# A three-layer routed-expert chain on one core: gate batches in pairs behind two slabs, and seams with row sums from the residual add and centred squares on ScalarE

## The reference, cut to what matters

```python
q = (xt @ w_q).reshape(T, PEER_HEADS, 2, PEER_HALF)
s = jnp.einsum('thpd,hpkd->thpk', q, sub_keys)
s_top, i_top = lax.top_k(s, PEER_TOPK)
...
best, pos = lax.top_k(cand, PEER_TOPK)
eid = jnp.take_along_axis(cand_id, pos, axis=-1)
gate = jax.nn.softmax(best, axis=-1)
act = jax.nn.gelu(jnp.einsum('td,thkd->thk', xt, u_tab[eid]), approximate=False)
out = jnp.einsum('thk,thkd->td', gate * act, v_tab[eid])
```

```python
h = layer_norm(DN_ALPHA * h + mix, ln_g, ln_b)   # (x - mean) * rsqrt(var + 1e-5) * g + b
n = rmsnorm(h, g)                                # x * rsqrt(mean(x*x) + 1e-6) * g
```

## Time and profile before

| | |
|---|---|
| median of 3 runs | 3086.1 us (3082.06 to 3093.37) |
| profiled execution | 3086.6 us, its span 3084.8 us |
| mean granted TensorE clock | 0.985 of full speed |
| busy in the span | PE 2974.1 us (96%), DVE 2069.3 (67%), ACT 1598.8 (52%), POOL 927.5 (30%) |
| chain that ended last | PE 87%, DVE 6%, ACT 2%, POOL 2% |
| DMA | 508.56 MB, 165 GB/s in the mean |

### The profile page before, as it was taken

The page is one execution under the profiler, slowest core; times in us unless marked ns, Lnnn a source line. Parts: engine busy times, 40 slices in busy tenths (PEclk is TensorE's granted clock), DMA queues, the critical chain, the costliest instruction groups (busy, mean ns, idle before and its releaser), DMA issues.

```text
span 3084.8 us, 66506 instructions
## 1 busy us (share of the span) xinstructions
PE 2974.1 (96%) x22893; PEld 2685.8 (87%) x22893; DVE 2069.3 (67%) x4318; ACT 1598.8 (52%) x2606; POOL 927.5 (30%) x378
## 2 busy tenths in 40 slices
PE   7899999999999989999999999899899999999998
PEld 6799999877788879999997778688799999977887
DVE  4369377888555554937788865675429477788755
ACT  3355443577454435553447755464545544477644
POOL 5578600000004647880000000155768820000000
PEclk9899999999999999999999999899999999999999
DMA  5345544455654325554445565443445544455564
GB/s 193 123 171 184 176 159 163 160 167 164 214 191 161 132 83 177 179 184 162 157 160 166 163 207 192 143 130 123 150 151 179 184 168 157 163 162 165 180 195 157
DMA packets 141401, 508.56 MB, mean 165 GB/s; under 512 B 16992, under 2 KB 18016, under 8 KB 140912
## 3 DMA queue, kind: packets, MB, share of 16 engines
q1 hardware_dynamic: 141296, 507.16, 49.8%
HBM read 506.05 MB, written 1.05 MB: 164 GB/s over the span
## 4 chain that ended last, share of the span: by engine, by line
PE 87%; DVE 6%; ACT 2%; POOL 2%; issue 1%; DMA 1%; SPq 1%; DVEq 0%; ACTq 0%; POOLq 0%
PE col L496 15%; PE col L498 14%; PE col L497 14%; PE acc L496 12%; PE acc L497 11%; PE acc L498 11%; PE acc L612 2%; PE col L612 2%; POOL w_lo L453 2%; ACT w_hi L717 1%; PE acc L581 1%; DVE work L1714 0%; DVE acc L958 0%; DVE pairs_of_gate L1144 0%; PE acc L1578 0%
## 5 line engine op out<-in xcount | busy, mean ns | idle before, releaser
L453 POOL TENSOR_TENSOR w_lo<-ring,w_hi 128x1024 fp32r<-128x1024 f32 x374 | 927.3, 2492 | 1560.5 <-ACT w_hi L717 1558.2
L717 ACT ACTIVATE w_hi<-ring 128x1024 fp32r<-128x1024 f32 x941 | 993.4, 1056 | 585.0 <-PE acc L498 477.4
L496 PE MATMUL col<-x_hi,w_hi 128*128 128x256 f32 (+1 forms) x3976 | 1143.0, 287 | 15.0 <-DVE x_lo L941 6.1
L497 PE MATMUL col<-x_lo,w_hi 128*128 128x256 f32 (+1 forms) x3976 | 1124.9, 283 | 0.0
L498 PE MATMUL col<-x_hi,w_lo 128*128 128x256 f32 (+1 forms) x3976 | 1123.6, 283 | 0.0
L453 DVE TENSOR_TENSOR w_lo<-ring,w_hi 128x1024 fp32r<-128x1024 f32 x567 | 692.1, 1221 | 221.4 <-ACT w_hi L717 221.4
L496 PEld LDWEIGHTS col<-x_hi,w_hi 128*128 128x128 f32 x3976 | 757.0, 190 | 22.3 <-issue 14.4
L498 PEld LDWEIGHTS col<-x_hi,w_lo 128*128 128x128 f32 x3976 | 757.5, 191 | 0.0
L497 PEld LDWEIGHTS col<-x_lo,w_hi 128*128 128x128 f32 x3976 | 753.8, 190 | 0.7
L496 PE MATMUL acc<-w_hi,c_hi 128*128 128x512 f32 x1664 | 668.3, 402 | 19.0 <-DVE c_lo L1049 10.3
L497 PE MATMUL acc<-w_lo,c_hi 128*128 128x512 f32 x1664 | 650.5, 391 | 0.0
(11 more groups left out here) (281 smaller groups left out, 2183.7 us busy)
## 6 DMA issues: line engine op xcount, KB each, us to landing
ring<-in_u SPq DMA_DIRECT2D x384, 512.0 KB, 3.2
ring<-in_v SPq DMA_DIRECT2D x384, 512.0 KB, 3.5
ring<-in_wq SPq DMA_DIRECT2D x48, 512.0 KB, 3.2
ring<-in_s_in SPq DMA_DIRECT2D x21, 512.0 KB, 3.5
ring<-in_c_in SPq DMA_DIRECT2D x16, 512.0 KB, 3.2
ring<-in_s_out SPq DMA_DIRECT2D x16, 512.0 KB, 3.5
ring<-in_s_gate SPq DMA_DIRECT2D x12, 512.0 KB, 3.5
ring<-in_s_conv SPq DMA_DIRECT2D x12, 512.0 KB, 3.5
```

The source lines that it names most:

```text
L453: eng.tensor_tensor(k.w_lo[s.slot][:, :], k.ring[s.slot][:, :], k.w_hi[s.slot][:, :].bitcast(F32), ALU.subtract).then_inc(k.lo[s.slot], 1)
L496: pe.matmul(out, a[0], b[0], start=start, stop=False, **kw)
L497: pe.matmul(out, a[0], b[1], start=False, stop=False, **kw)
L717: act.activation(k.w_hi[s.slot][:, :], k.ring[s.slot][:, :], ACT.Copy).then_inc(k.hi[s.slot], 1)
```

## The change

1. **Pairs.** In both passes PE takes two slabs and then two batches of gates. DVE's step takes two batches: both weighs, the one-hots of n+2 and n+3, then the splits (late: and coefficient rests) of slabs n+4 and n+5; the split of slab 3 goes ahead of the first weigh. The first late one-hots stand behind weigh 63.
2. **`row_tail`.** The third last slab is done whole; then tile 0 of the last two, then half 0 and then half 1 of tile 1. `tile_full` rises a second time when tile 1's half 0 is complete. The residual adds wait for each of these (`add_residual` now takes one half).
3. **Layer norm.** The residual add also gives its row sum (`accum_out`), from which a column operation makes the negative mean. ACT squares the centred rows (`centred_squares`), and their sums give the variance; the epsilon is the square root's bias. The two tiles' operations are interleaved on DVE by hand. ACT does four squares, two roots, and then the leads of slabs end+1 and end+2 (the latter behind `lead_x`, unless s is next).
4. **RMS seams.** DVE does all four residual adds first, then both norms (`finish_rms`). ACT squares both tiles ahead of the leads of end+1 and end+2.

```diff
@@ -615,17 +617,25 @@
         def gate_pass(late, slab):
-            for n in range(HEAD):
+            for n in range(0, HEAD, 2):
                 slab(n)
-                gates(Slab(n), late, wait=n >= SLOTS)
+                slab(n + 1)
+                for b in (n, n + 1):
+                    gates(Slab(b), late, wait=b >= SLOTS)
             with pe.Fori(0, TURNS - 1) as i:
-                for n in range(HEAD, HEAD + UNROLL):
+                for n in range(HEAD, HEAD + UNROLL, 2):
                     slab(n, i * 2)
-                    gates(Slab(n, i * 2), late)
-            for n in range(BATCHES - UNROLL, BATCHES - 1):
+                    slab(n + 1, i * 2)
+                    for b in (n, n + 1):
+                        gates(Slab(b, i * 2), late)
+            for n in range(BATCHES - UNROLL, BATCHES - 2, 2):
                 slab(n)
-                gates(Slab(n), late)
-            gates(Slab(BATCHES - 1), late)
+                slab(n + 1)
+                for b in (n, n + 1):
+                    gates(Slab(b), late)
+            slab(BATCHES - 2)
+            for b in (BATCHES - 2, BATCHES - 1):
+                gates(Slab(b), late)
             slab(BATCHES - 1)
     def row_tail(self, end):
         k, pe = self.k, self.pe
-        for t in range(NT):
...
-                if t == NT - 1:
-                    ins.then_inc(k.used, 1)
-            if t == 0:
-                ins.then_inc(k.tile_full, 1)
+        last = end - 1
+        self.row_slab(Slab(end - SLOTS))
+
+        def part(n, t, half):
+            slot = n % SLOTS
+            cut, cols = slice(t * P, (t + 1) * P), slice(half * 512, (half + 1) * 512)
+            return self.split_matmuls(k.acc[t * 2 + half][:, :], (k.c_hi[slot][:, cut], k.c_lo[slot][:, cut]),
+                                      (k.w_hi[slot][:, cols], k.w_lo[slot][:, cols]), False, n == last,
+                                      skip_group_check=True)
+
+        for n in (last - 1, last):
+            pe.wait_ge(k.coef[n % SLOTS], k.rows_in_slot(Slab(n), 1))
+            self.slab_ready(Slab(n))
+            for half in range(2):
+                ins = part(n, 0, half)
+        ins.then_inc(k.tile_full, 1)
+        for half in range(2):
+            part(last - 1, 1, half).then_inc(*((k.used, 1) if half else (k.half_done, 1)))
+            part(last, 1, half).then_inc(*((k.used, 1) if half else (k.tile_full, 1)))
-    def std(self, src, dst):
+    def std(self, src, dst, bias=0.0):
         k, act = self.k, self.act
         self.w.next(k.var)
-        act.activation(dst, src, ACT.Sqrt).then_inc(k.std, 1)
...
+        act.activation(dst, src, ACT.Sqrt, bias=bias).then_inc(k.std, 1)
+
+    def centred_squares(self, t):
+
+        k = self.k
+        self.w.next(k.mean)
+        for half in range(2):
+            self.square(k.acc[t * 2 + half][:, :], 2 * t + half, bias=k.small[:, 20 + t:21 + t])
...
+        act.activation(view(k.big, JUNK, cols, p=rows), src, ACT.Square, bias=bias, accum_out=k.small[0:rows, 40 + n:41 + n])\
            .then_inc(k.sq, 1)
             self.tile_std(NT)
         self.split_lead(Slab(end))
         if name in RMS_AFTER:
-            self.tile_squares(0, bool(after))
-        else:
-            self.tile_std(0)
-        self.split_lead(Slab(end + 1))
-        self.split_lead(Slab(end + 2))
-        if name in RMS_AFTER:
-            self.tile_squares(1, bool(after))
+            for t in range(NT):
+                self.tile_squares(t, bool(after))
+            self.split_lead(Slab(end + 1))
+            self.split_lead(Slab(end + 2))
             if after:
                 self.lead_x(range(NT))
-        elif after != ("s",):
+            return
+        eps = k.small[:, 49:50]
+        for t in range(NT):
+            self.centred_squares(t)
+        for t in range(NT):
+            self.tile_std(t, eps)
+        if after != ("s",):
+            self.split_lead(Slab(end + 1))
             self.lead_x([0])
-            self.tile_std(1)
             self.lead_x([1])
+            self.split_lead(Slab(end + 2))
         else:
-            self.tile_std(1)
+            self.split_lead(Slab(end + 1))
+            self.split_lead(Slab(end + 2))
             for t in range(NT):
                 self.tile_squares(t, True)
             self.lead_x(range(NT), meta=True)
...
-    def add_residual(self, t, last, alpha, ready=None):
+    def add_residual(self, t, half, last, alpha, sums=False, ready=None):
         k, dve, own = self.k, self.dve, self.own
-        if t == 0:
+        if half == 0:
             self.w.next(k.tile_full)
-        else:
+        elif t:
             dve.wait_ge(k.used, last + 1)
-        for half in range(2):
-            acc = k.acc[t * 2 + half][:, :]
-            ins = dve.scalar_tensor_tensor(acc, k.h[:, t, half * 512:(half + 1) * 512], alpha, acc, ALU.mult, ALU.add)
-            if half == 0 or ready is None:
-                own.do(ins)
+        acc = k.acc[t * 2 + half][:, :]
+        ins = dve.scalar_tensor_tensor(acc, k.h[:, t, half * 512:(half + 1) * 512], alpha, acc, ALU.mult, ALU.add,
+                                       accum_out=k.small[:, 16 + 2 * t + half:17 + 2 * t + half] if sums else None)
         if ready is None:
-            own.join()
+            own.do(ins)
         else:
             ins.then_inc(ready, 1)
...
-        for t in range(NT):
-            self.add_residual(t, last, DN_ALPHA)
-            for half in range(2):
-                own.do(dve.bn_stats(stats[:, t, half, :], k.acc[t * 2 + half][:, :]))
+        means = self.w.count(k.mean)
+
+        def residual(t, half):
+            self.add_residual(t, half, last, DN_ALPHA, sums=True)
+
+        def minus_mean(t):
             own.join()
-            own.do(dve.bn_aggr(mean_var[:, t, :], stats[:, t, :, :].rearrange("p h s -> p (h s)")))
-            own.join()
...
-            if t == 0:
-                self.w.next(k.param[slot], 32)
-            for half in range(2):
-                acc = k.acc[t * 2 + half][:, :]
-                own.do(dve.scalar_tensor_tensor(acc, acc, mean_var[:, t, 0:1], gain[:, half * 512:(half + 1) * 512],
-                                                ALU.subtract, ALU.mult))
+            dve.tensor_scalar(k.small[:, 20 + t:21 + t], k.small[:, 16 + 2 * t:17 + 2 * t],
+                              k.small[:, 17 + 2 * t:18 + 2 * t], -1.0 / D, ALU.add, ALU.mult).then_inc(k.mean, 1)
+            self.w.skip(k.mean, 1)
+
+        def centre(t, half):
+            self.w.next(k.sq)
+            dve.wait_ge(k.mean, means + t + 1)
+            acc = k.acc[t * 2 + half][:, :]
+            own.do(dve.scalar_tensor_tensor(acc, acc, k.small[:, 20 + t:21 + t], gain[:, half * 512:(half + 1) * 512],
+                                            ALU.add, ALU.mult))
+
+        def variance(t):
+            dve.tensor_scalar(k.small[:, 4 + t:5 + t], k.small[:, 40 + 2 * t:41 + 2 * t],
+                              k.small[:, 41 + 2 * t:42 + 2 * t], 1.0 / D, ALU.add, ALU.mult).then_inc(k.var, 1)
+
+        residual(0, 0)
+        residual(0, 1)
+        minus_mean(0)
+        residual(1, 0)
+        self.w.next(k.param[slot], 32)
+        centre(0, 0)
+        residual(1, 1)
+        minus_mean(1)
+        centre(0, 1)
+        variance(0)
+        centre(1, 0)
+        centre(1, 1)
+        variance(1)
+        own.join()
+        scale(0)
+        scale(1)
...
+    def finish_rms(self, name, last):
+
+        k = self.k
+        slot = 0 if name == "s" else 1
+        for t in range(NT):
+            for half in range(2):
+                self.add_residual(t, half, last, 1.0, ready=k.rms_in if half else None)
+        for t in range(NT):
+            self.rms_norm(t, slot, name == "s")
...
         def early(n, i=None):
-            weigh(Slab(n, i), 0)
+            if n == 0:
+                split_rest(k, dve, Slab(late_u + SLOTS))
+            for b in (n, n + 1):
+                weigh(Slab(b, i), 0)
+            for b in (n + 2, n + 3):
+                if b < BATCHES:
+                    onehots(Slab(b, i), 0)
             if n + 2 < BATCHES:
-                onehots(Slab(n + 2, i), 0)
-            elif n + 2 == BATCHES:
+                for s in (n + 4, n + 5):
+                    split_rest(k, dve, Slab(late_u + s, i))
+            else:
                 onehots(Slab(0), 1)
-            if n < BATCHES - 1:
-                split_rest(k, dve, Slab(late_u + n + SLOTS, i))
...
+        def value(s):
+            split_rest(k, dve, s)
+            if s.turn is not None or s.base < first + BATCHES:
+                self.coef_rest(experts[:, s.index(first), :], s)
+
         def late(n, i=None):
-            weigh(Slab(n, i), 1)
+            if n == 0:
+                value(Slab(first + SLOTS))
+            for b in (n, n + 1):
+                weigh(Slab(b, i), 1)
+            for b in (n + 2, n + 3):
+                if b < BATCHES:
+                    onehots(Slab(b, i), 1)
             if n + 2 < BATCHES:
```

(28 more changed lines are left out.)

26 lines of the change are left out of this document (6 added, 20 removed).

## The result

The changed kernel took 3056.4 us (median of 4 runs, 3054.6 to 3062.3) beside 3085.0 for the kernel before (4 runs, 3082.1 to 3093.4): ratio 0.990, 95% interval 0.9886 to 0.9913. The forecast was 3055.5 in a range of 3043 to 3072. The profiled execution took 3062.3, the slowest of its four, with a span of 3060.5: 24.3 us less than the one of before.

What follows compares the result with a forecast made beforehand. The prediction took TensorE's stream, with the seams where it waits, as the bound; its terms summed to 31.1 us off the profiled 3086.6, giving 3055.5 us (chance 0.62), range 3043 to 3072.

Steps and rivals of the forecast that it cites:

- The switch: Gate passes: two gate blocks in a row save 0.09 us a pair, 16.7 us in all, bounds 0 and 22.
- Starts: Start of each early pass: slab 1 ahead of gates 0 covers TensorE's idle, 7.8 us gained, bounds 6 and 11.
- Hand-overs: Ends of the gate passes: VectorE's new order makes TensorE wait, 1.8 us lost early-to-late and 1.1 behind late passes.
- Rival d: Early-to-late hand-overs: the longer idle drops TensorE to 1.2 GHz in all three layers, 3060 us; chance 0.08.
- VectorE keeps up: Gate passes: VectorE needs 5.57 of 6.23 us per late pair, 5.13 of 6.42 early; spare 0.4, cost nil.
- Rival a: Late pass: VectorE becomes the bound if ScalarE's leads stand open, 3094 us with one, 3196 with both; chance 0.09.
- Rival b: Gate passes: pairs save nothing, as second-block waits or the slab-to-slab boundary cost what the switch did, 3072 us; chance 0.08.
- `row_tail`: Tails of row stages: the last slab's coefficients are needed 1.36 us later, which removes waits, 4.6 us gained together.
- Layer-norm seams: Seams behind ab, peer0 and c: fewer statistics and interleaved tiles gain 0.7 us each, 2.1 in all.
- Into s: Seam behind peer1: GpSimd's second split holds an SBUF addition for 1.96 us, 0.8 us lost; without the hold 1.5 gained.
- Behind s and the end: Seam behind s and kernel's end: adds first and squares ahead of leads gain 2.8 and 0.8 us.
- rival c: Seams and tails give nothing, as GpSimd holds small VectorE operations and accumulators cost 0.2: 9.5 us go, 3065 us; chance 0.13.

Runs made afterwards that it cites:

- e5: The changed kernel with TensorE's gate-pass loop cut behind a slab's 24 long matmuls instead of the gates' 24 short ones: 3049.7 us, ratio to before 0.9879.
- e2: The changed kernel with the pairs part undone (batches one by one), new row_tail and seams kept: 3075.8 us, ratio to before 0.9959.
- e3: The kernel before with row_tail's new order alone, norms and their order as before: 3091.2 us, ratio to before 1.0006.
- e6: The changed kernel with VectorE's order mended at both ends of a gate pass (weighs before split, coef_rest before late one-hots): 3049.1 us, ratio to before 0.9881.
- f3: The changed kernel with four more VectorE operations in each late pair, their results unread: 3148.2 us, ratio to before 1.0191.
- a0: The changed kernel unaltered, run again on a later occasion beside its parts: 3054.2 us, ratio to before 0.9887.

## Why the prediction was right, point by point

- **The switch.** The mechanism was right and the size was off. 0.09 x 186 = 16.7 was forecast and 11.3 measured, 12.8 with the odd early pass of before taken out. The 0.09 itself was about right: 0.08 late (6.36 - 6.28), 0.11 early (6.57 - 6.46). The step that failed is that the term had nothing for the turn of the loop, 0.09 in every third pair; with e5's 4.8 added the pairs give 17.6., from which the 0.79 came, lie outside the loop, so they could not show what its turn costs behind 24 short matmuls (e5). The estimate of 19.9 us by the Trainium skill ("TensorE: Matmul & The Clock Gate", LDWEIGHTS) is further off than the row's.
- **Starts.** 7.8 as forecast against the profile of before, 11.1 against e2's: that layers 1 and 2 kept full clock behind their idle was read from one execution, and the traces of e2 and e3 show half clock there. The upper bound of 11 was about right.
- **Hand-overs.** The order of VectorE's work was read rightly and the losses came out at 1.2 and 1.1 for 1.8 and 1.1. They were not the price of pairing: e6 takes them out. Rival d is out: the idle of 1.12 us left the clock at 1.00 in the five microseconds behind it in all three layers.
- **VectorE keeps up.** Right: 5.59 of 6.31 late (forecast 5.57 of 6.23), 146.91/182 x 6.49 = 5.24 early (forecast 5.13). f3 puts the room at 0.3 where 0.4 was given. Rival a is out, and f3 is what it would look like. Rival b is out as well: 6.28 for 6.36.
- **`row_tail`.** 4.4 for 4.6 in the profile after, but booked as if it stood alone; e3 shows that it is worth nothing without parts 3 and 4. And the step on c was wrong: it took the 1.38 us for VectorE in the earlier trace rows as lateness that six more matmuls would cover. It stood behind a `coef_rest` that took 2.52 us beside a GpSimd split, and in the new tail the last slab's is held so late that TensorE waits over 2 us for it in eight of twelve traces, where c loses 1.0 to 3.0 us in place of the 1.36 gained. That the profile after came near the sum was luck.
- **Layer-norm seams.** The term was twice too large, 2.1 for 1.0. The walk put tile 1's scale at E+5.35, +0.3 for accumulators; it came at E+5.87. The accumulator reads and the longer squares (0.69) are visible; how the 0.22 splits between them was not tried. The rest lies behind it: from the scale to the first matmul it is 3.62 us, where it was 3.43; TensorE now transposes both tiles in one go there, but whether that is the cause was not tried.
- **Into s.** This step failed. L1071 was to be held for two microseconds and wasn't: -0.8 forecast, +0.9 measured. The rule that a split holds such an addition stands (2.33 us in c); the walk had GpSimd start at E+5.0 and it started at E+5.9, while the addition came at E+8.1 and not E+7.5, so that it met the last 0.13 us of the first split. That it fell there was not foreseen, so the gain is luck; but the order of events is the same from one execution to the next: in the ten later traces of the new seams L1071 took 0.15 to 0.17 us. The question that the prediction left on the means is answered for this shape. In this seam, in all eleven traces with the new layer norms, the first mean (one column, one pointer scalar) starts inside a GpSimd split of 2.74 us and takes 0.21 us, as it does without one:

```profile
1963.37 2.74 POOL L455 TENSOR_TENSOR w_lo<-ring,w_hi 128x1024 fp32r<-128x1024 f32 x1 [581.61 <-ACT w_hi L730]
...
1965.19 0.21 DVE L1006 TENSOR_SCALAR small<-small 128x1 f32<-128x1 f32 x1
```

No split ran beside a variance.

- **Behind s and the end.** 3.1 and 0.9 for 2.8 and 0.8. With the tails and the layer norms this puts rival c out: seams and tails gave 10.3 us in the profile after.
- **Not in the prediction.** The held addition in c (-4.2 in this execution, nothing in seven others) and the half clock (+2.0). The total of 31.1 lies among the three measured differences, 28.6, 34.4 and 29.6, partly because errors of both signs met: the pairs and layer norms were booked 6.5 too high (5 with the odd early pass taken out), into s 1.7 too low, the starts up to 3.3 too low, and the half clock happened to help. The lower end of the range, 3043, is also 1.4 us below what its three named terms give (5.6, 3.2 and 2.3 from 3055.5: 3044.4).

## What to carry to other kernels

Price a pattern in the place where it will run: a pair outside a loop doesn't show what the loop's turn costs; here it cost 0.09 us behind 24 short matmuls, and nothing that shows behind 12 short ones or behind a slab. When work is reordered so that a producer finishes later, book it together with the consumer's order, since one without the other may be worth nothing. Before booking a wait as lateness, look at how long the awaited instruction took: 2.5 us for an operation that takes 0.43 elsewhere was a hold here, and the new order moved it rather than ended it. And at a hand-over, look at what stands ahead of the awaited instruction on its in-order engine before calling the idle a price of the change.

## What the runs showed of the hardware

- A VectorE operation of 128 x 8 numbers took 0.16 us when it started 0.04 us ahead of a GpSimd operation and 2.33 when it started 0.09 behind it; one of 128 x 256 numbers took 0.43 when it started 0.07 ahead and 2.61 when 0.01 behind. The Trainium skill ("SBUF — State Buffer", Who interferes with whom) says that an operation with two SBUF inputs contends with a GpSimd one that reads SBUF, and that "issue order, not op shape, decides who blocks"; the traces agree, and show that a seam's or a tail's time can hang on less than a tenth of a microsecond, in the same kernel.
- The clock behind a seam is not a property of the kernel. The same stretches of the same kernel, the start of c and the start of peer1, had granted clocks of 0.87 and 0.67 in the first execution:

```profile
952.00:965.00 13.00, 11.19 (x81) 0.87 0.26 83
...
1132.00:1145.00 13.00, 12.14 (x72) 0.67 0.26 82
```

and the other way round in a0:

```profile
952.00:965.00 13.00, 11.55 (x69) 0.67 0.25 83
1128.00:1141.00 13.00, 12.20 (x89) 0.87 0.29 91
```

In the balance of these two traces they are worth 1.4 and 1.8 us, so a term under that can't be read from one profile's seam without looking at its clock.
